# Retention's rotations on another engine, the bias table and the router in another form, in a six-block transformer kernel

## The chip, the cores and the metric

The kernel runs on one core of a Trainium2 chip. The metric is the device time of one launch in microseconds (us).

## The reference, cut to what matters

A sequence of 256 tokens with 1024 features goes through six layers in float32. Three things in it are touched by the change:

- **Retention (layer 0).** `q`, `k`, `v` and a gate come from one projection of width 6144. `q` and `k` (4 heads of 256 columns) are rotated before the scores: in each head the first 128 columns are `x1`, the others `x2`, and they become `x1*cos - x2*sin` and `x2*cos + x1*sin`.
- **The relative bias of diff_attention (in layers 3 and 6).** `bias[h, q, k] = rel_bias[h, bucket(q - k)]`, with 32 buckets and 8 heads. It depends on `q - k` alone, so one row of 384 numbers for each head holds all of it.
- **The router of the mixture of experts (twice).** Logits are `x @ w` with 20 columns (4 groups and 16 experts); the best group and its two best experts of each token are picked from them.

## The kernel before, in words

The weights stream from DRAM in "wide" blocks of 1024x512 (four pieces of 128x1024, 512 KB each), and each enters the products in two fp32r parts: ACT copies a piece to `high_w` (high_wide, L556), DVE subtracts it from the staged piece into `low_w` (low_wide, L921), and PE makes three products for each stationary 128x128 tile of x: high by high, high by low and low by high (three, L1662 to L1664). A block is 2 row tiles x 8 chunks x 3 = 48 products of 512 columns. While PE works on one block, ACT and DVE split the next. SP loads a piece when `low_w` of the same piece of the block before is made.

All engines go through the same list of stages (PLAN), each in its own program, in this order: the retention projection, in which `linear` takes six blocks (q, k and part of v), then the turn (PE transposes, into `qk`) of the rotated q, two more blocks, the turn of the rotated k, four blocks of the gate; retention itself; its output projection (`residual`); `prenorm`, `bias`, the turn of the normalised rows, and the first mixture of experts (`gated`, with `router` first). After shared keys and MoBA attention come a second `residual`, `prenorm`, turn and `gated`, this time with no `bias` stage between them. Then four layers with diff, hgrn and sgu mixers, cross attention and dense units.

- **Rotations.** POOL makes them (`rotate`, L468 to L473), six tensor_tensor operations of 128x1024 for q and six for k, while PE, ACT and DVE are in the blocks of the projection that come after those of q and k. `table` holds cos and sin, `tmp` the two products with sin.
- **Bias table.** In the stage `bias` PE waits for the late constants and makes eight products (bias_table, L2052), each a column of rel_bias broadcast to 128 stationary columns by the 33x384 table of buckets; ACT copies each to `proj` (L745); POOL sends these 128x3072 numbers to the DRAM tensor `skew` (L500) and reads them back with a stride of 384 (L503), which shifts row p by p columns.
- **Turn and its early half.** After a residual the prenorm is fused with it: rows of tile 0 are normalised and turned ("early", turn_early) before the last products of the residual. `turn` sets `early` only if the stage just before it in the list is that prenorm. For the first mixture of experts it is the bias stage, so both tiles are turned after it.
- **Router.** 32 fp32 products (L1819): x's 128x128 tiles stationary, once the high part and once the low part, and the 20 columns of w moving; each fp32 product has two records in the trace. PE waits first for all of xh and xl. DVE picks groups and experts from bank 7 (L1082 on).
- **Start.** SP's queue: x tile 0, ident, x tile 1, the four pieces of block 0. The gain comes over POOL's queue. DVE: mean and scale of tile 0, low_wide of piece 0, the low part of x (L934) of tile 0, mean and scale of tile 1, low_wide of pieces 1 to 3.

Of the kernel before, what the change touches and what calls it, by code (L numbers as in the profile page):

```python
# [26 lines left out]
P = 128  # L27
S = 256
# [76 lines left out]
def plan():  # L105
# [53 lines left out]
    add("bias")  # L159
# [88 lines left out]
def build(nc, dram, out):  # L248
    ctx = ExitStack()
    with ctx:  # L250
# [39 lines left out]
        skew = nc.dram_tensor("skew", (8 * P * 385,), F32).ap()  # L290

# [35 lines left out]
        def columns(s, i):  # L327
# [11 lines left out]
        x_in, gain_in, mem_in, table_in = [sem("x_in0"), sem("x_in1")], sem("gain_in"), sem("mem_in"), sem("table_in")  # L339
# [12 lines left out]
        rotated, used_router = sem("rotated"), sem("used_router")  # L352
        ret_scored, ret_masked, ret_done, ret_taken = (
            sem("ret_scored"), sem("ret_masked"), sem("ret_done"), sem("ret_taken"))
        bias_rows, bias_copied, skewed, unskewed = (
            sem("bias_rows"), sem("bias_copied"), sem("skewed"), sem("unskewed"))
# [31 lines left out]
        def _(sp):  # L388
# [40 lines left out]
        def _(pool):  # L429
# [14 lines left out]
            def load_gain(n):  # L444
                if n:
                    pool.wait_ge(normed, 2 * n)
                pool.dma_start(gain[:, :], dram["gains"][n:n + 1, :].broadcast_to([P, D])).then_inc(gain_in, 16)

            def setup():
                link(nc.gpsimd.memset(minus_half[:, :], -0.5))  # L450
                load_gain(0)
# [7 lines left out]
            def rotate(col):  # L459

                x = pv(6144)[:, :, col:col + 1024].rearrange("p t (h a c) -> p t h a c", h=RET_HEADS, a=2)
                x1, x2 = x[:, :, :, 0, :], x[:, :, :, 1, :]
                cos, sin = (table[:, o:o + S].rearrange("p (t h c) -> p t h c", t=T, h=1)
                            .broadcast_to([P, T, RET_HEADS, P]) for o in (1024, 1280))
                a, b = (tmp[:, o:o + 1024].rearrange("p (t h c) -> p t h c", t=T, h=RET_HEADS)
                        for o in (0, 1024))
                eng = nc.gpsimd
                link(eng.tensor_tensor(a, x1, sin, ALU.mult))  # L468
                link(eng.tensor_tensor(b, x2, sin, ALU.mult))
                link(eng.tensor_tensor(x1, x1, cos, ALU.mult))  # L470
                link(eng.tensor_tensor(x2, x2, cos, ALU.mult))
                link(eng.tensor_tensor(x1, x1, b, ALU.subtract))
# [1889 lines left out]
```

## Time and profile before

| | us |
|---|---|
| median of 3 runs | 2882.65 (2880.4 to 2883.88) |
| profiled execution, its own time | 2882.81 |
| span of the profiled execution | 2881.0 |
| PE busy | 2703.5 (94%) |
| DVE busy | 1767.1 (61%) |
| ACT busy | 1449.0 (50%) |
| POOL busy | 95.6 (3%) |

The span is the time between the first and the last record; the execution's own time is 1.81 us longer. Busy shares are averages over stages with different limits. A PE record's end is modelled, so successive products are best read by the distance between their starts. The granted clock of PE is a share of full speed: 1.00 is 2.4 GHz and 0.50 is 1.2 GHz.

### The profile page before, as it was taken

How to read it: one execution, taken by the hardware profiler on the slowest of the kernel's cores; microseconds unless marked ns; L12 is line 12 of the kernel's file. 1: busy time of each engine (PE TensorE's matmuls, PEld its weight loads, DVE VectorE, ACT ScalarE, POOL GpSimd, SP SyncE). 2: the span in 40 equal slices, each digit the busy share in tenths (PEclk: the TensorE clock that was granted, in tenths of full speed). 3: DMA queues.
4: the chain of work that ended last, by engine and by line, in shares of the span. 5: the costliest groups of instructions: out<-in, count | busy, mean ns of one | idle time of the engine just before them, and what ended most of it. 6: DMA issues, size and time to landing. Idle time of an engine off the chain costs nothing.

```text
span 2881.0 us, 39077 instructions
## 1 busy us (share of the span) xinstructions
PE 2703.5 (94%) x12660; PEld 2213.3 (77%) x12660; DVE 1767.1 (61%) x2424; ACT 1449.0 (50%) x2043; POOL 95.6 (3%) x99
## 2 busy tenths in 40 slices
PE   7988999989799997899999989999999999999998
PEld 5766777768678776787887888788778887778886
DVE  5544888966598885655544665555555555564554
ACT  4443766755377664554444525444544544554443
POOL 3200000000000001000000000000000000000000
PEclk9997999999799998999999999999999999999999
DMA  5444888954398894354554405465453654443653
GB/s 199 166 141 146 289 318 315 344 193 139 132 348 320 314 330 133 103 183 155 189 195 139 147 1 183 131 212 183 159 174 129 209 194 148 159 131 127 206 189 107
DMA packets 149571, 546.03 MB, mean 190 GB/s; under 512 B 16662, under 2 KB 16838, under 8 KB 149329
## 3 DMA queue, kind: packets, MB, share of 16 engines
q1 hardware_dynamic: 144432, 525.47, 52.8%
q0 software_dynamic: 4752, 17.99, 2.1%
q8 instruction: 72, 1.18, 0.2%
q10 hardware_dynamic: 272, 1.05, 0.1%
q14 instruction: 43, 0.34, 0.0%
HBM read 541.81 MB, written 2.62 MB: 189 GB/s over the span
## 4 chain that ended last, share of the span: by engine, by line
PE 81%; DVE 10%; ACT 3%; issue 3%; DMA 2%; POOL 1%; DVEq 0%; SPq 0%; POOLq 0%; ACTq 0%
PE bank L1662 23%; PE bank L1664 23%; PE bank L1663 22%; DVE low_w L921 3%; PE bank L1740 2%; DMA stage_w<-in_wide 1%; PE bank L2106 1%; PE bank L1850 1%; DVE low_d L927 1%; PE bank L1863 1%; PE bank L2152 1%; PE bank L2168 1%; PE bank L1819 1%; PE bank L2076 1%; ACT tmp L761 1%
## 5 line engine op out<-in xcount | busy, mean ns | idle before, releaser
L921 DVE TENSOR_TENSOR low_w<-stage_w,high_w 128x1024 fp32r<-128x1024 f32 x784 | 960.1, 1242 | 417.4 <-ACT high_w L556 390.3
L1662 PE MATMUL bank<-high_w,xh 128*128 128x512 f32 x2624 | 1055.7, 402 | 44.1 <-DVE low_w L921 18.0
L1664 PE MATMUL bank<-high_w,xl 128*128 128x512 f32 x2624 | 1030.6, 393 | 0.0
L1663 PE MATMUL bank<-low_w,xh 128*128 128x512 f32 x2624 | 1030.3, 393 | 0.0
L556 ACT ACTIVATE high_w<-stage_w 128x1024 fp32r<-128x1024 f32 x784 | 821.9, 1058 | 239.6 <-PE bank L1664 220.7
L1662 PEld LDWEIGHTS bank<-high_w,xh 128*128 128x128 f32 x2624 | 497.8, 190 | 166.2 <-issue 36.8
L1664 PEld LDWEIGHTS bank<-high_w,xl 128*128 128x128 f32 x2624 | 497.5, 190 | 107.3
L1663 PEld LDWEIGHTS bank<-low_w,xh 128*128 128x128 f32 x2624 | 498.6, 190 | 97.7 <-issue 0.5
L927 DVE TENSOR_TENSOR low_d<-stage_d,high_d 128x1024 fp32r<-128x1024 f32 x216 | 255.5, 1223 | 45.7 <-ACT high_d L563 45.7
L1662 PE MATMUL bank<-high_d,hidden_h 128*128 128x512 f32 x576 | 224.8, 390 | 2.8 <-DVE low_d L927 2.8
L1664 PE MATMUL bank<-high_d,hidden_l 128*128 128x512 f32 x576 | 224.3, 389 | 0.0
L1663 PE MATMUL bank<-low_d,hidden_h 128*128 128x512 f32 x576 | 224.1, 389 | 0.0
L563 ACT ACTIVATE high_d<-stage_d 128x1024 fp32r<-128x1024 f32 x216 | 216.7, 1052 | 5.3 <-PE bank L1664 5.1
L1253 DVE TENSOR_TENSOR hidden_l<-bank,hidden_h 128x512 fp32r<-128x512 f32 x40 | 27.7, 692 | 190.8 <-ACT hidden_h L711 190.8
L711 ACT ACTIVATE hidden_h<-bank 128x512 fp32r<-128x512 f32 x40 | 23.9, 599 | 215.9 <-PE bank L1956 215.9
L441 POOL TENSOR_TENSOR stat<-stat,minus_half 128x1 f32<-128x1 f32 (+3 forms) x47 | 39.1, 832 | 2685.5 <-DVE stat L955 2200.3
L1662 PEld LDWEIGHTS bank<-high_d,hidden_h 128*128 128x128 f32 x576 | 108.1, 188 | 25.8 <-issue 3.6
L1664 PEld LDWEIGHTS bank<-high_d,hidden_l 128*128 128x128 f32 x576 | 108.1, 188 | 22.5
L1663 PEld LDWEIGHTS bank<-low_d,hidden_h 128*128 128x128 f32 x576 | 108.2, 188 | 22.2
L569 ACT ACTIVATE xh<-bank 128x512 fp32r<-128x512 f32 x88 | 48.5, 593 | 121.0 <-PE bank L1740 120.8
L597 ACT ACTIVATE proj<-bank 128x512 f32 (+1 forms) x53 | 31.7, 598 | 151.0 <-PE bank L1664 150.8
L934 DVE TENSOR_TENSOR xl<-bank,xh 128x512 fp32r<-128x512 f32 x88 | 57.0, 686 | 70.6 <-ACT xh L569 70.5
(250 smaller groups left out, 1934.5 us busy)
## 6 DMA issues: line engine op xcount, KB each, us to landing
stage_w<-in_wide SPq DMA_DIRECT2D x784, 512.0 KB, 4.7
stage_d<-in_down SPq DMA_DIRECT2D x216, 512.0 KB, 4.5
gain<-in_gains POOLq DMA_DIRECT2D x20, 512.0 KB, 4.9
skew<-proj POOLq DMA_DIRECT2D x1, 1536.0 KB, 6.8
h<-in_x SPq DMA_DIRECT2D x2, 512.0 KB, 5.9
proj<-in_hg_consts POOLq DMA_DIRECT2D x1, 1024.0 KB, 5.1
proj<-skew POOLq DMA_DIRECT2D x1, 1024.0 KB, 6.5
tmp<-in_mem POOLq DMA_DIRECT2D x1, 1024.0 KB, 6.8
```

The source lines that it names most:

```text
L441: nc.gpsimd.tensor_tensor(stat[:, at:at + n], stat[:, at:at + n], minus_half[:, :].broadcast_to([P, n]), ALU.pow).then_inc(rooted, 1)
L556: act.activation(high_w[:, w], stage_w[:, w], ACT.Copy).then_inc(split_hw, 1)
L563: act.activation(high_d[:, w], stage_d[:, w], ACT.Copy).then_inc(split_hd, 1)
L569: act.activation(part(xhv, b, chunk), part_bank(b), ACT.Copy).then_inc(kept_h, 1)
L597: act.activation(out_v[:, 0, columns(s, i)], bank[4][:, :], func).then_inc(taken[0], 1)
L921: vec.tensor_tensor(low_w[:, w], stage_w[:, w], high_w[:, w].bitcast(F32), ALU.subtract)\
L927: vec.tensor_tensor(low_d[:, w], stage_d[:, w], high_d[:, w].bitcast(F32), ALU.subtract)\
L934: vec.tensor_tensor(part(xlv, b, chunk), part_bank(b), part(xhv, b, chunk).bitcast(F32), ALU.subtract).then_inc(kept_l, 1)
L1662: pe.matmul(o, hi, wh, start=start, stop=False)
L1663: pe.matmul(o, hi, wl, start=False, stop=False)
L1664: return pe.matmul(o, lo, wh, start=False, stop=stop)
L1740: mm = pe.transpose(bank[2 * t + i][:, k * P:(k + 1) * P], src[:, t, (4 * i + k) * P:(4 * i + k + 1) * P], ident[:, :])
```

## The change

Three parts. **Rotations:** DVE makes the same twelve operations, cut in steps: two ahead of its work on each of blocks 3, 4 and 5 of the first `linear` (q), three ahead of each of the two blocks of the second (k). **Bias table:** the buckets and rel_bias are loaded at the start on SP's queue, as is now the gain of the first norm; one product gives 8x384, DVE negates it into `qk`, POOL sends it to DRAM (`bias_dram`), and a second DMA reads each row 128 times from there and writes `skew`. The stage `bias` is gone; the reading back stays, after retention. **Router:** ACT and DVE split the 128x160 router weights into `hidden_h` and `hidden_l` during the residual before; PE makes 3 fp32r products for each chunk and tile, the 20 columns stationary and x's 128 tokens moving (48 in all), waits for x in halves of a tile, ACT copies the 20x128 logits of each tile, and PE transposes them back into bank 7.

```diff
@@ plan
     prenorm()
-    add("bias")
     turn("norm", "s")
@@ sync
             for t in range(T):
                 sp.dma_start(hv[:, t, :], dram["x"][t * P:(t + 1) * P, :]).then_inc(x_in[t], 16)
                 if t == 0:
+                    sp.dma_start(gain[:, :], dram["gains"][0:1, :].broadcast_to([P, D])).then_inc(gain0_in, 16)
                     sp.dma_start(ident[:, :], dram["ident"]).then_inc(ident_in, 16)
+                    sp.dma_start(tmp[0:33, 0:384], dram["buckets"]).then_inc(bias_in, 16)
+                    sp.dma_start(tmp[0:33, 384:392], dram["rel_bias"]).then_inc(bias_in, 16)
@@ gpsimd
-            def rotate(col):
...
-            def retention():
...
             def skew_bias():
-                pool.wait_ge(bias_copied, 8)
-                rows = proj[:, 512:512 + 8 * 384].rearrange("p (h j) -> p h j", h=8)
+                pool.wait_ge(bias_copied, 1)
+                pool.dma_start(bias_dram.rearrange("(h j) -> h j", h=8), qk[0:8, 1024:1408]).then_inc(bias_out, 16)
+                pool.wait_ge(bias_out, 16)
+                rows = bias_dram.rearrange("(h a j) -> h a j", h=8, a=1).broadcast_to([8, P, 384])
                 pool.dma_start(skew.rearrange("(h p j) -> h p j", h=8, j=385)[:, :, 0:384], rows).then_inc(skewed, 16)
@@ scalar
+            def high_router(s):
+                m = PLAN[PLAN.index(s) + 3]
+                if m.kind == "gated" and m.moe is not None:
+                    act.wait_ge(late_in, 64)
+                    act.activation(hidden_h[:, 0:KC * ROUTER], table[:, ROUTER0 + m.moe * KC * ROUTER:][:, 0:KC * ROUTER],
+                                   ACT.Copy).then_inc(router_high, 1)
             def residual(s):
...
+                high_router(s)
                 square(nxt, 0)
...
                 if s.kind == "turn":
+                    if s.src == "q rotated":
+                        act.wait_ge(skewed, 16)
...
+                        for t in range(T):
+                            act.wait_ge(logits_turned, 2 * s.moe + t + 1)
+                            act.activation(tmp[0:ROUTER, 1024 + t * P:1024 + (t + 1) * P], bank[6 - t][0:ROUTER, t * P:(t + 1) * P],
+                                           ACT.Copy).then_inc(logits_kept, 1)
@@ vector
+            def rotate(n, steps):
...
+                for step in steps:
+                    if step == 0:
+                        dve.wait_ge(table_in, 16)
+                        for t in range(T):
+                            dve.wait_ge(taken[t], 2 * (n + 1))
+                        vec.tensor_tensor(a, x1, sin, ALU.mult)
...
                 def one(i):
+                    if s.width == 6144 and isinstance(i, int):
+                        if s.out == 0 and i >= 3:
+                            rotate(0, range(2 * (i - 3), 2 * (i - 2)))
+                        elif s.out == 6:
+                            rotate(1, range(3 * i, 3 * i + 3))
...
             mean(PLAN[1], 0)
             scale(PLAN[1], 0)
             low_wide(0, 0)
+            dve.wait_ge(bias_rows, 1)
+            vec.tensor_scalar(qk[0:8, 1024:1408], bank[7][0:8, 0:384], -1.0, None, ALU.mult).then_inc(bias_copied, 1)
             keep_early(PLAN[1])
@@ tensor
             def router(s):
-                for t in range(T):
-                    for i, part in enumerate((xhv, xlv)):
-                        for k in range(KC):
-                            w = table[:, ROUTER0 + (s.moe * KC + k) * ROUTER:][:, 0:ROUTER]
-                            mm = pe.matmul(bank[7][:, t * ROUTER:(t + 1) * ROUTER],
-                                           part[:, k, t * P:(t + 1) * P].bitcast(F32), w,
-                                           start=i == 0 and k == 0, stop=i == 1 and k == KC - 1)
+                pe.wait_ge(router_low, s.moe + 1)
+                for t in range(T):
+                    x = slice(t * P, (t + 1) * P)
+                    for b in range(2):
+                        pe.wait_ge(kept_h, kept(s.turn - 1) + 2 * t + b + 1)
+                        pe.wait_ge(kept_l, kept(s.turn - 1) + 2 * t + b + 1)
+                        for k in range(4 * b, 4 * b + 4):
+                            w = slice(k * ROUTER, (k + 1) * ROUTER)
+                            mm = three(bank[6 - t][0:ROUTER, x], hidden_h[:, w], hidden_l[:, w], xhv[:, k, x], xlv[:, k, x],
+                                       k == 0, k == KC - 1)
+                    mm.then_inc(logits_turned, 1)
+                for t in range(T):
+                    pe.wait_ge(logits_kept, 2 * s.moe + t + 1)
+                    mm = pe.transpose(bank[7][:, t * ROUTER:(t + 1) * ROUTER], tmp[0:ROUTER, 1024 + t * P:1024 + (t + 1) * P],
+                                      ident[0:ROUTER, 0:ROUTER])
                 mm.then_inc(used_router, 1)
             def bias_table():
-                pe.wait_ge(late_in, 96)
-                pe.wait_ge(ret_taken, 2 * RET_HEADS)
-                for j in range(8):
-                    if j >= 2:
-                        pe.wait_ge(bias_copied, j - 1)
-                    pe.matmul(bank[6 + j % 2][:, 0:384], proj[0:33, 384 + j:385 + j].broadcast_to([33, P]),
-                              proj[0:33, 0:384], start=True, stop=True).then_inc(bias_rows, 1)
+                pe.wait_ge(bias_in, 32)
+                pe.matmul(bank[7][0:8, 0:384], tmp[0:33, 384:392], tmp[0:33, 0:384], start=True, stop=True)\
+                    .then_inc(bias_rows, 1)
```

## Rows read from the trace of the kernel before

**Rows 1.** The page, part 4: the chain that ended last, by engine.
```profile
PE 81%; DVE 10%; ACT 3%; issue 3%; DMA 2%; POOL 1%; DVEq 0%; SPq 0%; POOLq 0%; ACTq 0%
```

**Rows 2.** Timeline, ACT: first start, us, engine, line, operation; in brackets idle before.
```profile
47.52 0.60 ACT L597 ACTIVATE proj<-bank 128x512 f32 x1 [4.47 <-PE bank L1664]
...
64.78 0.60 ACT L597 ACTIVATE proj<-bank 128x512 f32 x1 [10.85 <-PE bank L1664]
...
75.66 0.60 ACT L597 ACTIVATE proj<-bank 128x512 f32 x1 [4.47 <-PE bank L1664]
...
92.94 0.60 ACT L597 ACTIVATE proj<-bank 128x512 f32 x1 [10.87 <-PE bank L1664]
```

**Rows 3.** Timeline, POOL: first and last of the six rotations of q.
```profile
43.73 3.21 POOL L468 TENSOR_TENSOR tmp<-proj,table 128x1024 f32<-128x1024 f32 x1 [26.17 <-DVE proj L991]
...
58.60 3.25 POOL L473 TENSOR_TENSOR proj<-proj,tmp 128x1024 f32<-128x1024 f32 x1
```

**Rows 4.** Timeline, DVE: splitting three pieces in three blocks.
```profile
49.88 9.73 DVE L921 TENSOR_TENSOR low_w<-stage_w,high_w 128x1024 fp32r<-128x1024 f32 x3 [5.20 <-ACT high_w L556]
...
67.14 3.95 DVE L921 TENSOR_TENSOR low_w<-stage_w,high_w 128x1024 fp32r<-128x1024 f32 x3 [4.21 <-ACT high_w L556]
...
107.97 3.95 DVE L921 TENSOR_TENSOR low_w<-stage_w,high_w 128x1024 fp32r<-128x1024 f32 x3 [5.77 <-ACT high_w L556]
```

**Rows 5.** Groups of DVE by shape: busy us in total, mean ns of one.
```profile
L1563 DVE TENSOR_TENSOR proj<-proj,table 128x1024 f32<-128x1024 f32 x2 | 2.4, 1218 | 0.0
```

**Rows 6.** Timeline, DVE and PE, ahead of the first mixture of experts.
```profile
246.10 1.28 DVE L970 SCALAR_TENSOR_TENSOR y<-h,stat,gain 128x1024 f32<-128x1024 f32 x1 [0.66 <-POOL stat L441]
...
245.69 8.04 PE L2052 MATMUL bank<-proj 33*128 33x384 f32 x12 [3.02 <-ACT proj L745]
253.67 3.68 PE L1740 MATMUL bank<-ident,y 128*128 128x128 f32 x16
258.80 3.57 PE L1819 MATMUL bank<-table,xh 128*128 128x20 f32 x16 [1.46 <-ACT xh L569]
```

**Rows 7.** The same ahead of the second.
```profile
733.74 1.97 PE L1740 MATMUL bank<-ident,y 128*128 128x128 f32 x8 [5.02 <-DVE y L970]
737.17 3.57 PE L1819 MATMUL bank<-table,xh 128*128 128x20 f32 x16 [1.46 <-ACT xh L569]
...
747.40 3.58 PE L1819 MATMUL bank<-table,xl 128*128 128x20 f32 x16
...
732.40 1.28 DVE L970 SCALAR_TENSOR_TENSOR y<-h,stat,gain 128x1024 f32<-128x1024 f32 x1 [0.66 <-POOL stat L441]
...
736.38 0.69 DVE L934 TENSOR_TENSOR xl<-bank,xh 128x512 fp32r<-128x512 f32 x1 [0.16 <-ACT xh L569]
...
751.11 0.20 DVE L1082 TENSOR_TENSOR stat<-bank,stat 128x40 f32<-128x40 f32 x1 [13.93 <-PE bank L1819]
```

**Rows 8.** Windows: stretch, its length, busy us (count) of each engine, granted clock, DMA.
```profile
733.00:747.00 14.00, 11.80 (x55) 11.43 (x55) 3.32 (x12) 1.19 (x2) 0.57 (x1) 0.50 0.54 183
```

**Rows 9.** The chain in order of time: start, us until the next, what.
```profile
18.71 0.43 PE bank L1663
...
98.28 1.75 PE bank L1740 x16
```

**Rows 10.** Groups of ACT by shape.
```profile
L774 ACT ACTIVATE proj<-bank 128x128 f32<-128x128 f32 x24 | 6.3, 262 | 0.0
```

**Rows 11.** Timeline of the start, DVE, and the chain there.
```profile
9.84 1.28 DVE L970 SCALAR_TENSOR_TENSOR y<-h,stat,gain 128x1024 f32<-128x1024 f32 x1 [4.26 <-DMA gain<-in_gains]
...
13.44 1.28 DVE L934 TENSOR_TENSOR xl<-bank,xh 128x512 fp32r<-128x512 f32 x2
...
2.14 9.04 DMA stage_w<-in_wide
```

**Rows 12.** The page, part 6: DMA issues, KB each, us from issue to landing.
```profile
stage_w<-in_wide SPq DMA_DIRECT2D x784, 512.0 KB, 4.7
...
skew<-proj POOLq DMA_DIRECT2D x1, 1536.0 KB, 6.8
```

More of the change, by code:

```diff
@@ L457, in load_retention @@
                 pool.dma_start(table[:, :], dram["ret_table"]).then_inc(table_in, 16)
-            def rotate(col):
[L461 to L472, printed above, removed]
-                return eng.tensor_tensor(x2, x2, a, ALU.add)
-            def retention():
-                pool.wait_ge(table_in, 16)
-                for n in range(2):
-                    for t in range(T):
-                        pool.wait_ge(taken[t], 2 * (n + 1))
-                    rotate(n * 1024).then_inc(rotated, 1)
-                    pool.wait_ge(rotated, n + 1)
             def after_retention(s):
@@ L526, in _ @@
                     after_retention(s)
+                    unskew_bias()
                 elif s.kind in ("prenorm", "between") and s.norm >= 1:
                     load_gain(s.norm + 1)
[L529 to L530 removed]
                 if s.kind == "between":
@@ L977, in norm @@
                     scale(s, t)
+            def rotate(n, steps):
+                x = pv(6144)[:, :, n * 1024:n * 1024 + 1024].rearrange("p t (h a c) -> p t h a c", h=RET_HEADS, a=2)
+                x1, x2 = x[:, :, :, 0, :], x[:, :, :, 1, :]
+                cos, sin = (table[:, o:o + S].rearrange("p (t h c) -> p t h c", t=T, h=1)
+                            .broadcast_to([P, T, RET_HEADS, P]) for o in (1024, 1280))
+                a, b = (tmp[:, o:o + 1024].rearrange("p (t h c) -> p t h c", t=T, h=RET_HEADS) for o in (0, 1024))
+                for step in steps:
[4 more added lines that the diff above has]
+                        vec.tensor_tensor(a, x1, sin, ALU.mult)
+                    elif step == 1:
+                        link(vec.tensor_tensor(b, x2, sin, ALU.mult))
+                    elif step == 2:
+                        vec.tensor_tensor(x1, x1, cos, ALU.mult)
+                    elif step == 3:
+                        link(vec.tensor_tensor(x2, x2, cos, ALU.mult))
+                    elif step == 4:
+                        vec.tensor_tensor(x1, x1, b, ALU.subtract)
+                    else:
+                        vec.tensor_tensor(x2, x2, a, ALU.add).then_inc(rotated, 1)
             def linear(s):
                 out_v = pv(s.width)
-                if s.norm == 4 and s.width == 3072:
-                    dve.wait_ge(skewed, 16)
                 def one(i):
+                    if s.width == 6144 and isinstance(i, int):
[3 more added lines that the diff above has]
+                            rotate(1, range(3 * i, 3 * i + 3))
                     for p in range(WP - 1):
@@ L994, in linear @@
                 peeled = s.blocks - after(s).early
-                if peeled > 1:
+                if s.width == 6144 and not s.func:
+                    for i in range(peeled):
+                        one(i)
+                elif peeled > 1:
                     with dve.Fori(0, peeled) as i:
@@ L1026, in residual @@
                 i = 2 * s.halves - 1
+                m = PLAN[PLAN.index(s) + 3]
+                if m.kind == "gated" and m.moe is not None:
+                    dve.wait_ge(router_high, m.moe + 1)
+                    w = slice(0, KC * ROUTER)
+                    vec.tensor_tensor(hidden_l[:, w], table[:, ROUTER0 + m.moe * KC * ROUTER:][:, w],
+                                      hidden_h[:, w].bitcast(F32), ALU.subtract).then_inc(router_low, 1)
                 add(0, 1, i)
@@ L1940, in gated @@
                     return
-                wait_kept(s.turn - 1)
-                pe.wait_ge(late_in, 96)
+                pe.wait_ge(late_in, 64)
                 router(s)
@@ L2213, in _ @@
                     turn_stage(s)
-                elif s.kind == "bias":
-                    bias_table()
                 elif s.kind == "gates":
```

44 lines of the change are left out of this document (19 added, 25 removed).

## The prediction

> **What bounds the kernel now.** I read the chain that ended last first: PE holds 81% of it, DVE 10% [rows 1]. So an edit gains only where it shortens PE's work or a wait of PE, and I looked for the places where PE's steady rhythm breaks around the three touched stages. Through all of it the sum is made against the profiled execution's own 2882.81 us, which stands 0.16 above the median of the runs, so a difference carries over unchanged. About 0.2% (5.8 us) is what a measurement of this kernel can tell from no change.
>
> **Rotations: -12.8.** ACT takes tile 0 of each block when PE ends its first half, so the distance of these rows is the length of a block. From 64.78 to 75.66 it is 10.88 us; but it is 17.26 from 47.52 to 64.78 and 17.28 from 75.66 to 92.94 [rows 2]. In the first of these two long blocks POOL is rotating q, from 43.73 to 61.85 [rows 3], and the two with k repeat the pattern. What turned long is DVE's splitting: three pieces take 9.73 us then and 3.95 otherwise, a small wait included [rows 4]. PE waits for the fourth piece before it can begin the next block. So POOL's rotations cost nothing on POOL and 6.38 + 6.40 = 12.78 us on PE, by way of DVE. With POOL quiet this goes.
>
> What it costs on DVE: twelve operations of two SBUF inputs and 128x1024 outputs, for which the row is 1.22 us [rows 5]. Two are put ahead of each of three blocks (2.4 us) and three ahead of each of two (3.7 us). There DVE sits idle for 5.20 us in a q block, and 5.77 us in a block after a turn, before ACT hands it the next piece [rows 4] (the 4.21 us of the middle row follow a long block and still hold 3.7). All five fit, with at least 0.5 us to spare; the last step for q is made a block before PE's transposes want it. I take 0. If an operation took 2.4 us, two would still fit and three would be 7.2 - 5.5 = 1.7 late, twice: +3.4 as an upper bound. The cover is ACT's wait for PE to release a piece, which stays.
>
> **Bias table: -7.9.** Here the second mixture of experts is the model for the first, because its turn already has the early half and no bias stage. DVE's scale of tile 1 starts at 246.10 and 732.40, a shift of 486.30 [rows 6, 7]. The second's router starts at 737.17, which is 250.87 in the first's time; the first's starts at 258.80 [rows 6, 7]. The difference, 7.93 us, is all of the stage: the eight products of 8.04 us, six of them behind one another, and the eight transposes that now come early, less the wait for the normalised rows that takes their place (what is late next: PE's 5.02 us idle for DVE's y [rows 7]). Eight early transposes are added inside the residual at 0.87 us; they are counted, since the scale rows I align lie behind them on PE's side only; bounds 7.0 to 7.9. ACT's eight copies go too, off the path. POOL's two big DMAs were off it as well.
>
> **Router: -7.6 each, -15.2.** Before, PE's transposes of tile 1 end at 733.74 + 1.97 = 735.71, the router starts when the last xl is there, at 737.17, and DVE reads the logits at 751.11 [rows 7]. After, tile 0's xh and xl were kept long ago, so its 24 products start at 735.71. The halves of tile 1 are ready at about 736.4 + 0.7 = 737.1 [rows 7], before tile 0's products end, so they wait for nothing. The length of 48 products is then the open term. The clock granted from 733 to 747 is 0.50, 1.2 GHz [rows 8], after PE's idle 5.02 us, and a full PE with 20-column products did not lift it; I keep 1.2 GHz.
>
> No fp32r product of 128 moving columns stands in the trace. The nearest row at that clock: 512 columns in 0.43 us [rows 9], one column a cycle; a quarter is 0.107. The nearest of 128 columns is the transposes at full clock, 1.75 / 16 = 0.109 us, that is 262 cycles for 128 stationary and 128 moving columns [rows 9]: as if loading and moving were in succession, or at two cycles a column. With 20 columns to load at two cycles each that gives 40 + 128 = 168 cycles, 0.14 us. I take 0.14: 48 x 0.14 = 6.7 us. Ends: 0.053 (full clock) to 0.43 (no gain from being short, or fp32's four cycles a column).
>
> Then the tail that is new: ACT copies 20x128 in about 0.26 [rows 10], PE transposes once in 1.97 / 8 = 0.25, and three hand-overs of 751.11 - (747.40 + 3.58) = 0.13 [rows 7], with 0.2 for draining: 1.1 us. Tile 0's copy lies beside tile 1's products. DVE reads at 735.71 + 6.7 + 1.1 = 743.5 instead of 751.11: -7.6. Splitting the router's weights costs 0.3 us each on ACT and DVE inside the residual, where both wait for PE as in the projection; it is off the path, and so is the table load of ACT's Exp, which moves behind its copies but has DVE's ranking beside it.
>
> The Trainium skill weighs this term otherwise (TensorE: Matmul & The Clock Gate, section Back-to-back issue gap): cold, successive products are N / 1.2 ns apart, which for 128 is 107 ns. It agrees with the 512-column row (0.43) and leaves out any load time. By it the sum would be 2 x 48 x 0.033 = 3.2 us lower, 2844.7, as an estimate. The same page (LDWEIGHTS) gives a load of P / 1.2 ns, 107 for 128 columns; the router's own products, 20 moving columns by 128 stationary, are 3.57 / 16 = 0.22 us apart [rows 7], so for 4-byte weights the row is twice the rule.
>
> **Start: +1.0.** PE's first block hangs on piece 0, issued at 2.14 and landed 9.04 us later [rows 11], twice the usual 4.7 [rows 12]: it queued behind x, gain and ident. Three more issues of 0.43 go ahead of it on SP's queue, the bytes in all barely grow, and the gain, which DVE waited for until 9.84, comes first. I take 0.4 of 1.3. DVE gets one operation between splitting piece 0 and xl [rows 11]; scaled from 0.69 for 512 columns [rows 7] it is 0.52, and what follows it on DVE (xl, scale, three splits) is what PE waits for. The small product fills a time when PE has nothing yet. Bounds: 0 to +2.
>
> **POOL and DMA.** POOL now waits for the 12 KB to land and sends 1.5 MB to `skew` at about 20 us; only its load of the next gain is behind it, wanted at 230. ACT and DVE wait for it at the first turn, which comes near 86 us, 50 us later. Beside it the weights stream: 6.8 us of DMA [rows 12] against a room of about 10.88 - 1.22 = 9.7 us between splitting a piece and its next use, less the 4.7 of a load. I take 0, at most +2. Nothing downstream fills the time won: while the router runs, loads stand still with full buffers, so the mixture starts its units the same way, only earlier.
>
> **Sum.** -12.8 - 7.9 - 15.2 + 1.0 = -34.9; 2882.8 - 34.9 = 2847.9, forecast 2848.
>
> **Rivals.**
> 1. *Short fp32r products run at fp32's rate*, four cycles a column: 0.427 at 1.2 GHz, 48 x 0.427 = 20.5, DVE reads at 757.3, and each router is 6.2 slower than before: 2848 + 96 x 0.287 = 2875.5. For it: no short fp32r product is in the trace, and transposes show more than one cycle a column. Against: long ones show one cycle, and the one short product that is dear (20 columns in 0.22) is explained by its load of 256 cycles. Chance 0.2. Two cycles (0.213) would give 2848 + 96 x 0.073 = 2855; chance 0.1.
> 2. *Rotations crowd DVE*, or the slow splitting was not POOL's doing. The first: up to +3.4 to +12 if operations with a broadcast table last 2.4 to 3.2 us as on POOL, 2851 to 2860. The second would leave 12.8: 2861. The long splits lie inside POOL's rows to the microsecond. Chance 0.07.
> 3. *Slower*: a product pays four cycles a column and, unhidden, a full 128-column load of 256 cycles whatever its 20 columns: 0.43 + 0.21 = 0.64 us. 48 of them are 30.7 us, and the time is 2848 + 96 x 0.5 = 2896. It ends above before from 0.14 + 34.9 / 96 = 0.50 us a product. The row against it: 512-column products 0.43 apart hide their loads wholly. Chance 0.03.
>
> The forecast, 2839 (full clock in the router: 96 x 0.087 = 8.4 lower) to 2853, has 0.6.
>
> **Numbers.** To leave out no more than 2 in 10, the range reaches from 2839 to rival 1: 2877. Faster by over 0.2% means below 2876.9: the forecast, rival 2 and most of rival 1, 0.88; within, part of rival 1 and mishaps, 0.07; slower, rival 3 and leftovers, 0.05.
>
> **What would show it.** Blocks of 10.88 us throughout the projection, with splits of 1.2 us and DVE's rotations in its idle time; no L2052-like row near 245, and the first router starting some 9 us after PE's last residual product; 48 products at 0.14 us, each router from transposes to DVE's read in 7.8 us. I am wrong in size if products are not 0.1 to 0.2 us apart, and wrong in mechanism if DVE's splits stay at 3.2 us or PE waits for DVE in the projection.

## The result, and the profile after

The changed kernel takes 2843.77 us, the median of 4 runs (2838.93 to 2846.76), where the kernel before took 2882.41 beside it; the ratio is 0.9864 [0.9851, 0.9878]. That is 38.6 us less, and 4.2 less than the forecast of 2848. The profiled execution lasted 2846.76 us by its own time, with a span of 2845.0 against 2881.0: 36.0 less.

The page of the changed kernel, parts 1, 4, 5 and 6:

```profile
span 2845.0 us, 38945 instructions
...
PE 2681.7 (94%) x12618; PEld 2198.6 (77%) x12618; DVE 1766.0 (62%) x2439; ACT 1446.9 (51%) x2041; POOL 59.3 (2%) x85
...
PE 82%; DVE 9%; ACT 3%; issue 3%; DMA 1%; POOL 1%; DVEq 0%; POOLq 0%; ACTq 0%; SPq 0%
...
L905 DVE TENSOR_TENSOR low_w<-stage_w,high_w 128x1024 fp32r<-128x1024 f32 x784 | 944.2, 1221 | 404.8 <-ACT high_w L536 377.7
...
skew<-bias_dram POOLq DMA_DIRECT2D x1, 1536.0 KB, 14.3
```

The chain has its old shape: PE 82%, DVE 9% [rows 1]. The 784 splits of weight pieces now average 1221 ns, so none is slow any more. The last line shows a time that I had taken over as 6.8 us [rows 12]: the 1.5 MB that go from DRAM to `skew` land after 14.3.

**The projection.** ACT's timeline in the changed kernel, where it takes tile 0 of each block:

```profile
35.08 0.60 ACT L574 ACTIVATE proj<-bank 128x512 f32 x1 [4.47 <-PE bank L1690]
45.99 0.60 ACT L574 ACTIVATE proj<-bank 128x512 f32 x1 [3.58 <-PE bank L1690]
56.87 0.60 ACT L574 ACTIVATE proj<-bank 128x512 f32 x1 [4.47 <-PE bank L1690]
67.75 0.60 ACT L574 ACTIVATE proj<-bank 128x512 f32 x1 [4.47 <-PE bank L1690]
78.63 0.60 ACT L574 ACTIVATE proj<-bank 128x512 f32 x1 [4.47 <-PE bank L1690]
91.29 0.60 ACT L574 ACTIVATE proj<-bank 128x512 f32 x1 [5.28 <-PE bank L1690]
102.17 0.60 ACT L574 ACTIVATE proj<-bank 128x512 f32 x1 [4.49 <-PE bank L1690]
```

The first distances are 10.91, 10.88, 10.88 and 10.88 us. From 78.63 to 91.29 the turn of q lies between, and the last distance, in the blocks with three operations of a rotation, is 10.88 again. The two blocks of 17.3 us [rows 2] are gone. DVE's timeline, around a block with two operations of a rotation and one with three (L905 are the splits, the others operations of the rotation):

```profile
53.94 1.22 DVE L978 TENSOR_TENSOR tmp<-proj,table 128x1024 f32<-128x1024 f32 x1
55.08 1.22 DVE L980 TENSOR_TENSOR tmp<-proj,table 128x1024 f32<-128x1024 f32 x1
...
59.30 3.88 DVE L905 TENSOR_TENSOR low_w<-stage_w,high_w 128x1024 fp32r<-128x1024 f32 x3 [3.00 <-ACT high_w L536]
...
101.62 1.22 DVE L988 TENSOR_TENSOR proj<-proj,tmp 128x1024 f32<-128x1024 f32 x1
...
104.51 3.95 DVE L905 TENSOR_TENSOR low_w<-stage_w,high_w 128x1024 fp32r<-128x1024 f32 x3 [1.67 <-ACT high_w L536]
```

A rotation operation takes 1.22 us on DVE, as [rows 5] said, and after three of them DVE still waits 1.67 us for ACT. No block is longer for the rotations.

**The first router.** PE's timeline in the changed kernel, with the first products, the two around the change of pace, and the last:

```profile
235.11 1.97 PE L1766 MATMUL bank<-ident,y 128*128 128x128 f32 x8 [5.01 <-DVE y L957]
236.73 0.45 PE L1688 MATMUL bank<-xh,hidden_h 128*20 128x128 f32 x1
236.98 0.31 PE L1689 MATMUL bank<-xl,hidden_h 128*20 128x128 f32 x1
237.09 0.31 PE L1690 MATMUL bank<-xh,hidden_l 128*20 128x128 f32 x1
...
239.86 0.31 PE L1689 MATMUL bank<-xl,hidden_h 128*20 128x128 f32 x1
...
240.14 0.22 PE L1689 MATMUL bank<-xl,hidden_h 128*20 128x128 f32 x1
240.20 0.22 PE L1690 MATMUL bank<-xh,hidden_l 128*20 128x128 f32 x1
...
241.10 0.22 PE L1690 MATMUL bank<-xh,hidden_l 128*20 128x128 f32 x1
241.26 0.24 PE L1854 MATMUL bank<-ident,tmp 20*128 20x20 f32 x1
241.68 0.23 PE L1854 MATMUL bank<-ident,tmp 20*128 20x20 f32 x1 [0.19 <-ACT tmp L858]
```

and DVE's, with the scale of tile 1 and the reading of the logits:

```profile
233.77 1.28 DVE L957 SCALAR_TENSOR_TENSOR y<-h,stat,gain 128x1024 f32<-128x1024 f32 x1 [0.67 <-POOL stat L446]
...
242.05 0.20 DVE L1104 TENSOR_TENSOR stat<-bank,stat 128x40 f32<-128x40 f32 x1 [3.50 <-PE bank L1854]
```

Products start 0.11 us apart (from 237.09 to 239.86, 2.77 us for 26 of them: 0.107), and from 240.1 on 0.06 apart (240.20 to 241.10, 0.90 for 15). All 48 take 4.5 us. From scale to logits it is 8.28 us; in the second mixture, whose scale starts at 700.93 and whose read at 709.41, it is 8.48, where before it was 18.71 [rows 7]. The pace changes with the clock, by the windows of the changed kernel (columns as in [rows 8]):

```profile
237.00:240.00 3.00, 3.00 (x31) 3.00 (x30) 1.39 (x10) 0.86 (x2) 0.00 (x0) 0.50 0.71 257
240.00:241.30 1.30, 1.30 (x22) 1.19 (x20) 0.00 (x0) 0.00 (x0) 0.00 (x0) 0.97 1.04 419
```

The granted clock is 0.50 (1.2 GHz) until 240 and nearly whole (2.4 GHz) after.

**Where the time went**, by stretches between DVE's scales and reads, in the two profiles (us):

| stretch | before | after | difference |
|---|---|---|---|
| start, to the scale of tile 1 | 15.44 | 13.87 | -1.6 |
| from there to the residual's first scale | 223.22 | 212.39 | -10.8 |
| first mixture, scale to logits (bias table and router) | 26.65 | 8.28 | -18.4 |
| second mixture, scale to logits (router) | 18.71 | 8.48 | -10.2 |
| second mixture, the rest (not touched) | 335.11 | 338.46 | +3.4 |
| the hgrn layer (not touched) | 203.78 | 206.99 | +3.2 |
| the memory's norm (not touched) | 13.71 | 15.05 | +1.3 |

The second row holds two things: the projection's blocks, 12.8 us shorter, and what follows retention, 2.0 us longer (1.7 of them in a group of sixteen transposes that is shown below). The four touched rows sum to -41.0 us, and to -43 without these 2.0. The span fell by 36.0, so what nobody touched gave back 5.0 net (the three rows shown lost 7.9, others won some). Whether that belongs to the change is the first thing to test.

### The profile page after: what moved, and what is told of

Same layout as the page of the kernel before. It is cut to its first block, busy times and chain, and to the rows that moved or that the text cites. A ratio compares the mean times of both kernels' runs of the same rounds, so it can differ in the third digit from the quotient of the medians.

```text
span 2845.0 us, 38945 instructions
## 1 busy us (share of the span) xinstructions
PE 2681.7 (94%) x12618; PEld 2198.6 (77%) x12618; DVE 1766.0 (62%) x2439; ACT 1446.9 (51%) x2041; POOL 59.3 (2%) x85
## 4 chain that ended last, share of the span: by engine, by line
PE 82%; DVE 9%; ACT 3%; issue 3%; DMA 1%; POOL 1%; DVEq 0%; POOLq 0%; ACTq 0%; SPq 0%
PE bank L1688 24%; PE bank L1690 23%; PE bank L1689 23%; DVE low_w L905 3%; PE bank L1766 2%; PE bank L1884 1%; PE bank L2135 1%; PE bank L1897 1%; DVE low_d L911 1%; PE bank L2181 1%; PE bank L2197 1%; ACT tmp L741 1%; DVE y L957 1%; PE bank L2105 1%; POOL stat L446 1%
## 5 line engine op out<-in xcount | busy, mean ns | idle before, releaser
L905 DVE TENSOR_TENSOR low_w<-stage_w,high_w 128x1024 fp32r<-128x1024 f32 x784 | 944.2, 1221 | 404.8 <-ACT high_w L536 377.7
L1766 PE MATMUL bank<-ident,y 128*128 128x128 f32 x336 | 49.7, 297 | 51.0 <-DVE y L957 42.7
## 6 DMA issues: line engine op xcount, KB each, us to landing
skew<-bias_dram POOLq DMA_DIRECT2D x1, 1536.0 KB, 14.3
```

The costliest lines, as they stand in the source:

```text
L905: vec.tensor_tensor(low_w[:, w], stage_w[:, w], high_w[:, w].bitcast(F32), ALU.subtract)\
L1766: mm = pe.transpose(bank[2 * t + i][:, k * P:(k + 1) * P], src[:, t, (4 * i + k) * P:(4 * i + k + 1) * P], ident[:, :])
```

## The experiments

**The changed kernel again.** No edit.

> The changed kernel once more, with a second profile, as the measure for the others of this call. Theory (stretches that no edit touches differ between executions because PE's granted clock falls and rises at other points of them): the same total within 0.3%, but single stretches between two norms differ from the first profile by 1 to 3 us, above all the two mixtures, the memory norm and the layer with hgrn. Rival (they differ because the kernels differ): all stretches repeat within 0.2 us.

It took 2842.34 us, 0.9861 [0.9844, 0.9878], with a span of 2839.7. The first router repeats (8.33 us from scale to logits), the second takes 7.45 instead of 8.48. The untouched stretches don't repeat either: the hgrn layer takes 203.81 instead of 206.99, the memory's norm 13.74 instead of 15.05, the second mixture's rest 336.64 instead of 338.46. PE's transposes ahead of the retention's output product show how, in the first profile of the changed kernel and then in this one:

```profile
181.34 3.65 PE L1766 MATMUL bank<-ident,proj 128*128 128x128 f32 x16 [1.50 <-DVE xl L918]
```

```profile
181.30 1.94 PE L1766 MATMUL bank<-ident,proj 128*128 128x128 f32 x16 [1.50 <-DVE xl L918]
```

The same sixteen transposes behind the same wait take 3.65 us at one clock level and 1.94 at the other. In the hgrn layer the granted clock is 0.93 on average in the first profile (206.99 us) and 0.95 in this one (203.81). A second profile of the kernel before, below, has 0.96 and 201.78 us there. So untouched stretches differ by 1 to 5 us between executions of one kernel, and single profiles can't assign less.

**Rotations back on POOL**, the rest as changed.

```diff
-                        if s.out == 0 and i >= 3:
-                            rotate(0, range(2 * (i - 3), 2 * (i - 2)))
-                        elif s.out == 6:
-                            rotate(1, range(3 * i, 3 * i + 3))
...
+                    retention()
```

> The changed kernel with the rotations of q and k back on POOL, the rest as changed. Theory (POOL's rotations slow DVE's splitting, and PE waits for it): the two blocks beside them last 17.3 us again instead of 10.9, DVE's splits there 3.2 us each instead of 1.2, and the time is 2843.8 + 12.8 = 2857 (ratio to before 0.991). Rival (the slow splitting belonged to something else of that stretch in the kernel before): blocks stay at 10.9, time 2844.

It took 2853.22 us, 0.9908 [0.9891, 0.9924], which is 10.6 above the run without an early turn below (2842.58 on the same chip, within noise of the changed kernel). Two blocks are long again: ACT takes tile 0 at 47.03 and 62.44 (15.41 us) and at 73.32 and 90.57 (17.25), together 10.9 over 2 x 10.88. POOL's and DVE's rows in the second of them:

```profile
75.28 2.40 POOL L473 TENSOR_TENSOR proj<-proj,table 128x1024 f32<-128x1024 f32 x1
77.76 3.24 POOL L474 TENSOR_TENSOR proj<-proj,table 128x1024 f32<-128x1024 f32 x1
81.08 3.24 POOL L475 TENSOR_TENSOR proj<-proj,tmp 128x1024 f32<-128x1024 f32 x1
```

```profile
75.68 9.72 DVE L931 TENSOR_TENSOR low_w<-stage_w,high_w 128x1024 fp32r<-128x1024 f32 x3 [5.20 <-ACT high_w L562]
```

Three splits take 9.72 us beside POOL's operations. In the q block they take 7.89 instead of 9.73 [rows 4], as much less as the block is shorter than 17.26; why, no run shows. The mechanism stands, and the rival that the slow splits had another cause falls.

**The old router in the changed kernel.** The fp32 products with x stationary come back, and so do their waits; the high and low halves of the weights and the copies of the logits go.

```diff
-                            mm = three(bank[6 - t][0:ROUTER, x], hidden_h[:, w], hidden_l[:, w], xhv[:, k, x], xlv[:, k, x],
-                                       k == 0, k == KC - 1)
...
+                            mm = pe.matmul(bank[7][:, t * ROUTER:(t + 1) * ROUTER],
+                                           part[:, k, t * P:(t + 1) * P].bitcast(F32), w,
+                                           start=i == 0 and k == 0, stop=i == 1 and k == KC - 1)
```

> The changed kernel with the old router: 32 fp32 products with x stationary, waiting for all of xh and xl, no split of the router's weights and no transposes back. Theory (the whole second gain of the mixture stages is the product form): from the start of DVE's scale of tile 1 to its reading of the logits 18.7 us in both mixtures instead of 8.3 and 8.5, the time 2843.8 + 2 x 10.3 = 2864 (ratio 0.994). Rival (part of it is given back later, because PE's clock comes out of the shorter router lower and the gathering products then run slower): the local 10.3 us stand but the time rises by less than 16 us, and the gathering products (32 records) take 5.2 us here against 6.05.

It took 2862.69 us, 0.9939 [0.9923, 0.9956], 20.1 above the same neighbour. PE's timeline, and the window over both tiles' products:

```profile
236.47 3.58 PE L1834 MATMUL bank<-table,xh 128*128 128x20 f32 x16 [1.46 <-ACT xh L549]
239.88 3.58 PE L1834 MATMUL bank<-table,xl 128*128 128x20 f32 x16
```

```profile
233.00:250.00 17.00, 15.50 (x72) 15.13 (x72) 2.62 (x11) 2.48 (x3) 0.59 (x1) 0.50 0.35 131
```

From scale to logits it is 18.72 and 18.71 us: the two routers are worth 10.4 and 10.2 us here, not 7.6. In the second, 1.8 of it is the earlier start behind the scale (2.96 us instead of 4.77), 9.1 the products (4.7 instead of 13.8), and the copies and the transposes back take 0.7 of it away. The clock stays at 0.50 through 13.6 us of back-to-back products with 20 moving columns, where it rose under the new ones.

**Every router product twice.** The second pass starts the sums anew; it adds 48 products to each router and nothing to what is computed.

```diff
-                    for b in range(2):
+                    for b in (0, 1, 0, 1):
```

> The changed kernel with each tile's 24 router products made twice, the second time over the first. Theory (a short product costs 0.105 us at 1.2 GHz and 0.06 at 2.4, nothing else): the 48 added products of each router run almost all at full clock and add 2.9 to 3.5 us. [...]

It took 2847.19 us in one run. From scale to logits it is 11.01 and 11.43 us, 2.7 and 2.9 more, so 48 added products cost 0.06 us each. The clock is low for the first 2.9 and 3.9 us, about as long as without them, so what is added runs at the whole clock. At 1.2 GHz an fp32r product of 128 columns pays one cycle a column (0.107 us are 128 cycles), at 2.4 GHz a little more (0.06 us are 144), and rivals 1 and 3 fall.

**No early turn for the first mixture.** A stage that does nothing stands between norm and turn, as the bias stage did.

```diff
     prenorm()
+    add("nothing")
     turn("norm", "s")
```

> The changed kernel with an empty stage between prenorm and turn of the first mixture, so that tile 0 is turned after the residual and not inside it. Theory (the 7.9 us of the bias part are the eight products; the early turn is worth little, because PE waits 5 us for tile 1 anyway and would turn tile 0 there): DVE reads the first logits 0 to 1 us later, time 2844 to 2845. Rival (the early turn carries a part of its own: eight transposes, and xh and xl of tile 0 which the router's products wait for): 2 to 3 us later, 2846 to 2847.

It took 2842.58 us, 0.9871 [0.9854, 0.9887]: no change. From scale to logits it is 8.13 us, no later than with the early turn. The eight transposes of tile 0 go back into the time in which PE waits for y. So what the bias table gave back was its own products on PE, and the early half was worth nothing.

**Why the start became earlier: the gain's load on POOL's queue.**

```diff
-                    sp.dma_start(gain[:, :], dram["gains"][0:1, :].broadcast_to([P, D])).then_inc(gain0_in, 16)
...
+                pool.dma_start(gain[:, :], dram["gains"][0:1, :].broadcast_to([P, D])).then_inc(gain0_in, 16)
```

> The changed kernel with the gain of the first norm on POOL's queue again instead of second on SP's. Theory (the start gained because the gain, on SP's queue ahead of x tile 1, no longer shares the transfers and DVE scales tile 0 at 6.3 instead of 9.8): DVE's scale of tile 0 at 9.8 again and PE's second piece of block 0 at 17.9 to 18.4 instead of 16.3 to 17.8; time 1 to 2 us longer. Rival (the start gains from something else, the order of the queue or chance): tile 0's scale comes late but PE's second piece is not later than 17.7.

It took 2841.53 us, 0.9863 [0.9835, 0.9891]. DVE's timeline:

```profile
6.79 1.28 DVE L957 SCALAR_TENSOR_TENSOR y<-h,stat,gain 128x1024 f32<-128x1024 f32 x1 [1.12 <-DMA gain<-in_gains]
```

The gain is still there 3 us before its old 9.84 [rows 11], and the scale of tile 1 comes at 14.07. The queue that issues the gain isn't the reason, and my theory fell. Yet the start that came earlier is not kept. ACT takes tile 0 of block 1 (the second block) at 32.87 here, against 35.08 in the first profile, and then it waits for the weights of block 2, which travel beside the transfer to `skew`:

```profile
36.48 1.06 ACT L536 ACTIVATE high_w<-stage_w 128x1024 fp32r<-128x1024 f32 x1 [3.00 <-DMA stage_w<-in_wide]
```

The next distance is 13.65 us, 2.8 over 10.88, and tile 0 of block 2 comes at 46.52 instead of 45.99.

**The kernel before, again**, without an edit:

> The kernel before, for a second profile. Theory (its late start is its own: gain, x and weights crowd each other): ACT squares x tile 1 at 9.9 us, takes weight piece 0 at 11.2, PE's second piece of block 0 starts at 17.9, each within 0.3. Rival (the start differs by chance as it does among profiles of the changed start, where the second piece came between 16.3 and 17.8): it starts before 17.5. Of the rest I expect the two long blocks of 17.3 and the bias stage again, and stretches that the change leaves alone shifted by 1 to 3 us.

**and the kernel before with two small loads in SP's queue**, between ident and x's tile 1. They are the loads that the change puts there for its 33x8 product. POOL waits for them before its rotations, which is not shown.

```diff
                     sp.dma_start(ident[:, :], dram["ident"]).then_inc(ident_in, 16)
+                    sp.dma_start(tmp[0:33, 0:384], dram["buckets"]).then_inc(early_in, 16)
+                    sp.dma_start(tmp[0:33, 384:392], dram["rel_bias"]).then_inc(early_in, 16)
```

> The kernel before with the two small loads of the bias table (buckets and rel_bias) put on SP's queue between ident and x tile 1, where the change has them, and used for nothing. Theory (they hold x tile 1 and the weights back by 0.8 us in the queue, and that lets the gain of POOL's queue through first, as in the changed kernel with the gain on POOL): gain lands by 7 us instead of 9.8 and PE's second piece starts at 16.3 to 17.8. Rival (the small loads only cost their 0.8 us): gain at 9 to 10 us, second piece at 18.5 or later.

They took 2876.86 and 2879.3 us, one run each. DVE's timeline, of the kernel before again and then with the small loads:

```profile
9.14 1.28 DVE L970 SCALAR_TENSOR_TENSOR y<-h,stat,gain 128x1024 f32<-128x1024 f32 x1 [3.45 <-DMA gain<-in_gains]
...
12.06 1.22 DVE L921 TENSOR_TENSOR low_w<-stage_w,high_w 128x1024 fp32r<-128x1024 f32 x1 [1.64 <-ACT high_w L556]
```

```profile
7.30 1.28 DVE L974 SCALAR_TENSOR_TENSOR y<-h,stat,gain 128x1024 f32<-128x1024 f32 x1 [1.64 <-DMA gain<-in_gains]
...
10.93 1.23 DVE L925 TENSOR_TENSOR low_w<-stage_w,high_w 128x1024 fp32r<-128x1024 f32 x1 [2.34 <-ACT high_w L560]
```

With the small loads the gain is taken 1.8 us earlier and the first weight piece split 1.1 earlier, in one profile each. The gain's part repeats: with these loads ahead of x's second tile DVE scales tile 0 at 6.3 to 7.3 us in every profile, without them at 9.1 and 9.8. The other part does not: in the profiles of the changed kernel with POOL's rotations and with the doubled router the scale of tile 1 comes at 15.04 and 15.27, as late as in the kernel before (15.44 and 15.21). The small loads are issued ahead of x's second tile and delay its issue by 0.8 us, and yet ACT has that tile at 8.57 us instead of 9.71; why is open. In the times nothing of it is seen (2879.3 against 2876.86).

The second profile of the kernel before also says how much of the table above is chance. It has its two blocks of 17.26 us and its mixtures of 26.64 and 18.72, but the residual's first scale comes at 235.98, not 238.66. Against it the two profiles of the changed kernel are 9.7 and 11.7 us earlier there, not 12.4 and 14.4.

**Square fp32r products.** 24 unused products, 128 stationary by 128 moving columns, stand ahead of each router; the rest is as changed.

```diff
                 pe.wait_ge(router_low, s.moe + 1)
+                for k in range(24):
+                    pe.matmul(bank[4][:, 0:P], xhv[:, k % KC, 0:P], xhv[:, (k + 1) % KC, 0:P], start=True, stop=True)
```

> The changed kernel with 24 fp32r products more ahead of each router, 128 stationary and 128 moving columns, into bank 4, used for nothing. They measure the term of the forecast that no row of the kernel before had. Theory (loading runs beside moving and costs two cycles a column, so that 128 stationary columns set 256 cycles): 0.213 us apart at 1.2 GHz, 0.107 to 0.115 at full clock. Rival (one cycle a column for both, side by side): 0.107 at 1.2 GHz, the same as with 20 stationary columns. Second rival (one after the other): 0.32 at 1.2 GHz.

It took 2856.92 us in one run. PE's timeline and the windows over the square products and over the router's behind them:

```profile
237.05 5.36 PE L1843 MATMUL bank<-xh 128*128 128x128 f32 x24
242.21 0.31 PE L1688 MATMUL bank<-xh,hidden_h 128*20 128x128 f32 x1
```

```profile
237.00:242.00 5.00, 5.00 (x26) 5.00 (x24) 1.50 (x10) 0.77 (x2) 0.00 (x0) 0.50 0.99 307
242.00:247.00 5.00, 5.00 (x48) 5.00 (x49) 0.00 (x0) 0.27 (x1) 0.00 (x0) 0.51 0.28 111
```

24 products from 237.05 to 242.21 are 0.215 apart, about 256 cycles at 1.2 GHz. That fits a load of 128 columns at two cycles each, with the product's own 128 cycles beside it and not behind: one after the other would be 0.32. With 20 columns to load (40 cycles) the product's 128 are what counts, and that is 0.107. One cycle a column for each, one after the other, would also give 256 cycles here, but 148 with 20 columns (0.123 us), and 0.107 came.

The same number parts the router's gain. The change swaps the roles of x and weights and replaces fp32 by three fp32r products at once. With x stationary, 48 fp32r products would take 48 x 0.215 = 10.3 us at 1.2 GHz, an estimate from these rows, against 13.8 before and 4.7 after. So more of the gain comes from the roles than from the type. No run has fp32 products with the roles swapped.

**Filling PE's idle time.** PE's clock is 0.50 in the router after PE waited 5.01 us for y. If the wait is the reason, work in it must lift the clock. Unused products of the identity with itself fill three such waits of each mixture: 20 ahead of tile 1's transposes, 5 ahead of the ranking, 22 behind it (each has two records in the trace).

```diff
+            def warm(n, b):
+                for _ in range(n):
+                    pe.matmul(bank[b][:, 0:P], ident[:, :], ident[:, :], start=True, stop=True)
...
+                    if s.src == "norm" and after(s).moe is not None:
+                        warm(20, 7)
```

> The changed kernel with products of ident by ident into banks that are free, where PE waits around the routers: 20 before tile 1's transposes, 5 before the ranking products, 22 after them. They leave the result as it is. Theory (PE's low clock after its waits costs the transposes, the router's products and the gathering products time): granted clock 1.00 through the router, 48 products in 2.9 us instead of 4.2, 32 gathering records in 3.7 instead of 6.1, about 5 us a mixture, time 2834. Rival (the fillers keep the clock up but delay what they stand before, or later stretches fall into the low clock instead): less than 4 us in all.

It took 2829.2 us (2827.99 to 2832.16), 0.9816 [0.9797, 0.9834]: 13.1 below the changed kernel on the same chip (2842.34), the fastest version of this study. PE's timeline, and the windows over the router and over the gathering of the chosen rows:

```profile
230.25 4.63 PE L1694 MATMUL bank<-ident 128*128 128x128 f32 x40
235.44 1.09 PE L1770 MATMUL bank<-ident,y 128*128 128x128 f32 x8 [0.56 <-DVE y L957]
```

```profile
234.10:240.20 6.10, 5.34 (x67) 4.90 (x67) 3.89 (x13) 2.19 (x6) 0.59 (x1) 1.00 0.76 236
249.00:254.00 5.00, 4.46 (x38) 4.27 (x38) 2.41 (x9) 1.42 (x3) 0.00 (x0) 1.00 0.01 3
```

The transposes take 1.09 us instead of 1.97, scale to logits 6.03 in both mixtures instead of 8.3 and 8.5, and the gathering 3.82 instead of 6.18. The gathering of the first mixture in the changed kernel's timeline:

```profile
252.17 6.18 PE L1884 MATMUL bank<-qk,y 128*128 128x128 f32 x32
```

With the second's (3.82 for 6.43) that is 4.6 and 5.1 us in the two mixtures, 9.7 in all, against the first profile of the changed kernel; against its second one, on the same chip as this run, it is 8.1. The other 3 to 5 of the 13 us lie in stretches without an added product, such as the hgrn layer (201.66 us against 203.81). That layer took 201.8 us also in profiles without any such product (with POOL's rotations 201.79, with the doubled router 201.80), so no run shows that the added products cause this part.

**The first 20 alone**:

> The changed kernel with only the first 20 of the idle products, those before tile 1's transposes, and none around the ranking. Theory (each group keeps its own stretch warm): from scale to logits 6.0 us as with all of them, but the gathering products at 6 us again, so that 2.3 of about 5 us a mixture are had: 2838 to 2840. Rival (the first group is enough, since the router then follows it warm and the ranking's wait is short): gathering at 3.8 us and 2829 to 2833.

2834.02 us, 0.9839 [0.9823, 0.9856], with 6.03 and 6.04 us to the logits but gatherings of 5.41 and 5.06: 6.8 us of local gain against the first profile instead of 9.7. The time lies between the two expectations. The hgrn layer took 201.76 us in this profile too.

**25 more ahead of the retention's transposes**:

```diff
+                warm(25, 4)
                 for m in range(2):
                     for t in range(T):
                         turn(s.turn + m, v[:, :, m * D:(m + 1) * D], t, (mixed, m + 1))
```

> The same with 25 such products more before the transposes of retention's output, where PE waits 6 us for DVE. Theory: those 32 transposes run at 0.109 us instead of 0.226, and the residual's first products at full clock too: 2 to 3 us less than the kernel without them, time 2831. Rival: no difference beyond 1 us.

2832.16 us, 0.9831 [0.9809, 0.9852]: nothing more. PE's timeline:

```profile
177.15 1.97 PE L1770 MATMUL bank<-ident,proj 128*128 128x128 f32 x16 [0.43 <-DVE proj L1339]
182.29 2.88 PE L1770 MATMUL bank<-ident,proj 128*128 128x128 f32 x16 [3.17 <-DVE xl L918]
```

The first sixteen halve (3.67 in the changed kernel), and PE then waits 3.17 instead of 1.50 us for DVE's xl. A faster PE in front of a wait for another engine gives nothing.

## Why the prediction was right, point by point

The sum was -34.9, and the time fell by 38.6 by the medians. The local terms came to more, about 43 against the one profile of before and some 3 less against the other. That the forecast is only 4.2 us off is in part luck: the routers gave 5 to 6 us more than their terms and the start up to 2.6, and untouched stretches and the weights of block 2 took part of it back.

**Rotations, -12.8: right.** The projection's blocks are 12.8 us shorter in the profile, the operations last 1.22 us on DVE, all of them fit, and with POOL back the slow splits come back. The term for POOL and the DMAs, put at 0 with at most +2, was too small: from tile 0 of block 1 to that of block 2 it was 10.88 to 13.65 us in the profiles with the new bias table, most where block 1 came early (13.04 with the old router, 13.65 with the gain on POOL's queue), so it cost 0 to 2.8. `skew` takes 14.3 us, so it meets the weights of block 2. ACT's timeline of the changed kernel's second profile:

```profile
36.57 1.06 ACT L536 ACTIVATE high_w<-stage_w 128x1024 fp32r<-128x1024 f32 x1 [1.72 <-DMA stage_w<-in_wide]
```

That distance was 11.66 us instead of 10.88 (34.25 to 45.91), 0.8 more; in the first profile it was 10.91. The five pieces issued between 20 and 40 us landed after 9.4 us at the median there (8.7 in the first profile), not 4.7, and the room I had counted was 9.7. I had also said that loads stand still while the router runs. The rows do not bear that out, neither before (DMA share 0.54 [rows 8]) nor after (0.71 and 1.04 in the windows above), but no cost of it is seen.

**Bias table, -7.9: right.** The first mixture now equals the second (8.28 and 8.48 us), where before they were 26.65 and 18.71, 7.9 apart. Its working spoke of an early half; the run without one shows that the products alone are the gain.

**Router, -7.6 each: the mis-sized term.** It gave 10.2 to 11.3. In the second mixture I forecast 11.1 us from scale to logits (732.40 to 743.5), and 8.48 came. The products are 2.0 of the difference (4.7 us, from 703.89 to 708.62, not 6.7), the tail 0.3 (0.8 instead of 1.1), the start 0.3 (2.96 us after the scale, not 3.31: I had added the transposes' modelled 1.97 us, and the next product starts 1.62 after they do). The products were shorter for two reasons. The step that failed first is the product's 0.14 us: I read the transposes' 262 cycles as loading and moving in succession, and the square products, with the 0.107 of the router's own, show them side by side, so 20 columns of load vanish behind 128 moving ones. At 1.2 GHz that is 0.107, 48 x 0.033 = 1.6 us. The Trainium skill had this number (TensorE: Matmul & The Clock Gate, Back-to-back issue gap: N / 1.2 ns cold, 107 ns for 128), and the trace agrees. The second is the clock that I kept: in the first mixture it rose 3.3 us into the products and took the last 18 of 48 to 0.06, in the second after 3.7 us, which is worth 0.4 to 0.6. In the second profile of the changed kernel it rose after 1.4 us in the second mixture, and the router gave 11.3. My evidence was that 20-column fp32 products never lifted it, which the old router confirms over 13.6 us; it did not carry over to the new ones.

**Start, +1.0: wrong in sign, by the scale of tile 1.** It was -1.6 in the profile, and between -0.2 and -1.6 over the others. I had DVE's added operation right (0.54 us, 0.52 predicted) and the landings wrong: I counted issues on SP's queue as delays, and x's second tile and the gain came earlier than before in spite of them. By block 2 it was gone or nearly so: its tile 0 comes at 45.9 to 47.0 us in the profiles of the new start, at 47.52 and 44.88 in the two of the kernel before.

**Untouched stretches, 0: unstated.** The prediction took them as fixed. They move by 1 to 5 us from one execution to another. In the first profile they gave back 5, which makes the sum look closer to the terms than it was.

**The rivals.** Four or two cycles a column (rival 1), crowding on DVE or slow splits without POOL (2), and 0.64 us a product (3) are all excluded by the rows above. The router's other bound was the full clock from the first product on. It came true for the last 18 products only.

## What to carry to other kernels

Where an engine is "only" beside the critical one, look at what its work does to the others' durations: POOL's rotations cost nothing on POOL and 12.8 us on PE, through DVE. For short products make the small operand stationary and the 128 columns moving: the load hides, and fp32r pays about one cycle a column. And where PE waits a few microseconds before a chain of short work, unused products in the wait can be worth something (here 4 to 5 us a mixture), provided that nothing else is late right behind.

## What the runs showed of the hardware

- Two-input VectorE operations that last 1.22 us take about 3.2 beside POOL's two-input ones, which last 2.4 to 3.4.
- Loading fp32r weights takes about two cycles a column, 0.215 us for 128 at 1.2 GHz, beside the product that runs. The Trainium skill's load (TensorE: Matmul & The Clock Gate, LDWEIGHTS: P / 1.2 ns, 107 for 128) is half of the measured; the measurement decides.
- After PE's 5 us of waiting the granted clock is 0.50, and how soon it rises differs. Under the router's products alone it rose after 3.3 us in the first mixture and 3.7 in the second, in another execution after 3.4 and 1.4. Behind 24 square products without a gap (5.2 us) it took 4.7 us of the router's in the first mixture and 3.2 in the second. Under 13.6 us of fp32 products with 20 moving columns it did not rise in any profile.
- The 12 KB from `qk` to DRAM landed 6.3 us after the issue, and the 1.5 MB spread from there after 14.3, twice the 6.8 us that the same bytes took from SBUF [rows 12]. But the 14.3 us were shared with the weights (DMA share 0.86 on average), and no weights were loaded beside the 6.8, so the two paths are not compared by it.
